# Attention steps of a hybrid decoder layer on one core: the prompt's turn ahead of the cached unit's turn

## The reference

```
# prompt: causal, in blocks of 128 queries, for each of 8 heads
s = (ql @ ckv.T + qr @ krope.T) * scale, masked
o = softmax(s) @ ckv

# sample: 4 new tokens a batch, 8 batches, over 4096 cached rows in pages of 128 and the new rows
s_past = q_lat @ ckv_past.T + q_rope @ krope_past.T
p = softmax(concat(s_past, s_new) * scale)
o = p[:P] @ ckv_past + p[P:] @ ckv_new
```

## Time and profile before

| what | value |
|---|---|
| median of 3 runs | 1400.43 us (1396.89 to 1400.48) |
| the profiled execution: its time | 1402.6 us |
| its span in the profile | 1400.6 us |
| TensorE busy | 1347.0 us, 96% |
| VectorE, ScalarE, GpSimd busy | 44%, 30%, 24% |
| mean granted clock of TensorE | 0.988 of full |

### The profile page before, as it was taken

One profiled execution on the slowest core, in us unless ns is written; L12 is line 12 of the kernel. 1 busy time (PEld: TensorE's weight loads), 2 busy tenths in 40 slices (PEclk: granted clock), 3 DMA queues, 4 the chain that ended last, 5 costly groups with the idle time before them and its releaser, 6 DMA issues.

```text
span 1400.6 us, 28560 instructions
## 1 busy us (share of the span) xinstructions
PE 1347.0 (96%) x11784; PEld 1250.5 (89%) x11784; DVE 614.8 (44%) x1020; ACT 418.0 (30%) x694; POOL 339.6 (24%) x351
## 2 busy tenths in 40 slices
PE   7999999999999999899999988889999999999997
PEld 6999998999999989667777666789999999999997
DVE  6245335234347995334444453355423333333334
ACT  5232221221234222322323333233422222222235
POOL 0219246128221112512222220031121021021022
PEclk9999999999999999999999999999999999999999
DMA  6223222222225213659999976442222222322321
GB/s 234 83 70 104 86 77 78 91 71 82 89 65 181 73 55 98 227 170 308 337 315 329 316 265 209 147 153 91 76 79 87 92 81 83 106 83 68 105 72 67
DMA packets 78932, 189.14 MB, mean 135 GB/s; under 512 B 10226, under 2 KB 13203, under 8 KB 78515
## 3 DMA queue, kind: packets, MB, share of 16 engines
q1 hardware_dynamic: 73762, 176.90, 38.1%
q10 hardware_dynamic: 3024, 6.69, 1.2%
q0 software_dynamic: 2048, 4.20, 0.9%
HBM read 178.06 MB, written 9.69 MB: 134 GB/s over the span
## 4 chain that ended last, share of the span: by engine, by line
PE 84%; DVE 7%; POOL 3%; ACT 2%; issue 2%; DMA 2%; SPq 0%; ACTq 0%; DVEq 0%; POOLq 0%
PE d L1676 59%; PE e L1965 8%; PE e L2018 2%; DVE w_lo L1086 2%; PE e L1999 2%; PE d L2049 2%; PE d L2028 1%; ACT w_hi L579 1%; PE d L2039 1%; PE e L2011 1%; PE e L2002 1%; PE e L1696 1%; PE d L1696 1%; PE e L1844 1%; DMA gate_m<-gates 1%
## 5 line engine op out<-in xcount | busy, mean ns | idle before, releaser
L1086 DVE TENSOR_TENSOR w_lo<-raw,w_hi 128x1024 fp32r<-128x1024 f32 (+2 forms) x191 | 223.6, 1170 | 390.0 <-ACT w_hi L579 389.1
L1676 PE MATMUL d<-x_hi,w_hi 128*128 128x272 f32 x1616 | 337.7, 290 | 9.0 <-DVE w_lo L1296 6.8
L1676 PE MATMUL d<-x_hi,w_lo 128*128 128x272 f32 x1616 | 335.4, 289 | 0.0
L1676 PE MATMUL d<-x_lo,w_hi 128*128 128x272 f32 x1616 | 334.4, 288 | 0.0
L579 ACT CAST w_hi<-raw 128x1024 fp32r<-128x1024 f32 (+2 forms) x191 | 185.7, 972 | 478.2 <-PE d L1676 447.8
L1676 PEld LDWEIGHTS d<-x_hi,w_hi 128*128 128x128 f32 x1616 | 255.4, 189 | 11.5 <-DVE w_lo L1296 6.8
L1676 PEld LDWEIGHTS d<-x_lo,w_hi 128*128 128x128 f32 x1616 | 255.1, 189 | 0.0
L1676 PEld LDWEIGHTS d<-x_hi,w_lo 128*128 128x128 f32 x1616 | 253.5, 190 | 0.0
L937 POOL TENSOR_TENSOR hid<-silu,up 128x544 f32<-128x544 f32 x42 | 56.9, 1356 | 499.3 <-DVE up L1159 487.4
L1676 PE MATMUL d<-hid_hi,w_hi 128*128 128x272 f32 x640 | 134.4, 291 | 4.8 <-DVE w_lo L1086 2.7
L1676 PE MATMUL d<-hid_hi,w_lo 128*128 128x272 f32 x640 | 132.4, 288 | 0.0
(11 more groups left out here) (346 smaller groups left out, 1861.4 us busy)
## 6 DMA issues: line engine op xcount, KB each, us to landing
kv<-kv_src SPq DMA_DIRECT2D x256, 256.0 KB
raw<-w_gu SPq DMA_DIRECT2D x87, 512.0 KB, 3.4
raw<-w_post SPq DMA_DIRECT2D x34, 512.0 KB, 3.4
raw<-w_d1b SPq DMA_DIRECT2D x16, 384.0 KB, 3.2
raw<-w_d2b SPq DMA_DIRECT2D x16, 384.0 KB, 3.2
raw<-w_in SPq DMA_DIRECT2D x10, 512.0 KB, 3.4
gate_m<-gates SPq DMA_DIRECT2D x16, 272.0 KB, 3.7
gates<-gate_m ACTq DMA_DIRECT2D x12, 272.0 KB
```

What stands on the lines that cost most here:

```text
L1086: nc.vector.tensor_tensor(w_lo[:, s % 2, 0:n, :], raw[:, raw_pos(s), 0:n, :], w_hi[:, s % 2, 0:n, :].bitcast(FP), ALU.subtract).then_inc(S ...
L1676: ins = mm(out[:, b, :], w[:, pos, c0 + k, :], x[:, k, b * HALF:(b + 1) * HALF], start=first, stop=stop)
```

## The change

In each step TensorE runs `turn(n - 1)` ahead of `unit_turn(n)` instead of behind it, and ScalarE runs `turned(n - 1)` ahead of `unit_turned(n)`. All else stays: `values(n - 2)` and `unit_values(n)` follow in the same order, and no buffer, wait or load is changed.

```diff
             nc.scalar.activation(p_p[:, n % 2, 0:w], d[:, 0, n % 2, 0:w], ACT.Exp, bias=astat[:, 0, n:n + 1],
                                  accum_out=astat[:, 1, n:n + 1]).then_inc(S.exp_done, 1)
-            unit_turned(n)
             if n >= 1:
                 turned(n - 1)
+            unit_turned(n)
...
             scores(n)
             for k in now[:1]:
                 job(k)
-            unit_turn(n)
             if n >= 1:
                 turn(n - 1)
+            unit_turn(n)
             if n >= 2:
                 values(n - 2)
             unit_values(n)
```

## The result

The changed kernel took 1400.97 us in the median (21 runs) against 1398.85 us (21 runs) of the kernel before, and the measured ratio is 1.0029, 95% interval 1.0016 to 1.0043. The ratio is taken over the fast runs alone, which leaves out one run of the changed kernel (2633.69 us). It is not the quotient of the two medians, which is 1.0015. The forecast of 1.0018 lies between the two and inside the interval, and 1400.97 us lies in the range I gave: the kernel is slower by about 0.3% or less. What the change costs is read from the profiles.

A forecast was written before the change was run, and what follows sets the result against it. TensorE, busy 96% of the span, was taken as the bound. Losses of 0.85 (i=2), 0.22 (n=1) and 1.39 us (n=22, 25, 26, 27) made +2.5 us: 1402.9 us, ratio 1.0018, range 1398.0 to 1406.0.

The forecast's parts named there:

- The chain of 1.07 us: From the unit's turn through copy L802 to the unit's values: 1.07 us that other TensorE work must cover.
- Cover by i: With i = n mod 4 setting block counts: cover suffices at i=0, 1, 3; i=2 short by 0.17 us, n=1 loses 0.22.
- ScalarE's order free: Putting the prompt's copy ahead of the unit's on ScalarE costs nothing itself.
- diag later than the exponentials: At n=22, 25, 26, 27 the prompt's turn waits for diag, 0.1 to 0.4 us behind the exponentials; nothing is hidden.
- rival 3: Waits for the exponentials shrink because the prompt's turn fills them: 1399.8 us, or 1398.2 with full clock at n=27; chance 0.06.
- n=22: Late step where TensorE waits: 0.26 us for diag plus 0.17 for lost cover, 0.43 us together.
- rival 2: Longer idle time at n=22 drops TensorE's clock too: 1404.5 to 1405.5 us; chance 0.16, shared with i=3 losing cover.
- a granted clock below full at n=22: Sign in the profile after that would show the forecast wrong: TensorE's clock below full in step 22.
- n=30 as zero: Step n=30 would add 0.17 us, but counted zero since n=31 waits 0.3 us for kv anyway.
- The lower bound of 1 us: Smallest loss, if a third of the handover is a modelling artefact and later waits take up part.
- L2018's waits at i=2: Sign of being right: the unit's values wait for L802 or ScalarE, 0.1 to 0.2 us each, 1 to 1.5 in all.
- The waits of L2039: Sign of being right: three or four waits for diag replace those for p_n at L2011, over 6.7 us in total.

The follow-up runs named there:

- e4: Changed kernel with values(n-2) also moved ahead of the unit's turn, so all cover is gone: 1425.52 us, ratio 1.0166, loop 287.91 us.
- e8: Changed kernel with the new order on both engines in steps 0 to 21 alone, the old one from 22 on: 1399.97 us, ratio 1.0010.
- e1: The changed kernel run again with no edit: 1405.12 us, ratio 1.0010, loop 268.20 us.
- e2: Kernel before with only TensorE's order changed, ScalarE still copying the unit first: 1406.26 us, ratio 1.0023, loop 268.30 us.
- e3: Kernel before with only ScalarE's order changed, TensorE still running the unit's turn first: 1411.03 us, ratio 1.0060, loop 272.78 us.
- e7: Changed kernel with the new order on both engines in steps 22, 25, 26 and 27 alone: 1399.71 us, ratio 1.0012.
- e10: Changed order with VectorE forming diag of step n early, in step n itself: ratio 0.9975, loop 266.44 us.
- e11: diag formed early on VectorE, new order in steps 22, 25, 26 and 27 alone, old order elsewhere: ratio 0.9987, loop 264.37 us.
- e5: The kernel before, unedited, profiled a second time: 1396.89 us, ratio 0.9997, loop 265.47 us.
- e6: The kernel before, unedited, profiled a third time: one run, 1399.42 us, loop 265.37 us.
- e9: Kernel before, old order, with VectorE forming diag of step n early, in step n itself: ratio 0.9974, loop 265.46 us.
- first pair: First profiles of the kernel before and the changed kernel, no further edit: loop 264.27 us before, 268.26 us after.

## Why the prediction was right, and where not

- **The chain of 1.07 us** was right to 0.01 us: 1.07 between the unit's turn and its values at n=1, 2, 6, 10, 14 and 18 of the changed kernel. It is no constant of the engines, though: behind `values` it was 1.18 (e4).
- **Cover by i** was right: no loss at i=0, 1 and 3, with the 0.05 us of spare at i=3 real, 0.15 to 0.17 us at i=2, 0.21 at n=1. Forecast 1.07 us for these together, measured 1.03; four of the five i=2 steps of e8 give 7.81 to 7.82 again.
- **ScalarE's order free** was right for the pair of edits (e1 against e2), and only for the pair (e3: +8.5 us in the loop).
- **diag later than the exponentials** was right, so rival 3 (faster) fell for the reason given. e7 has +0.43, +0.13 and +0.43 us at n=22, 25 and 26 as forecast; n=27 was +0.35 for +0.40 in the changed kernel (in e7 the clock hides it). e10 and e11 take the reason away, and three of the four steps get shorter in e11, two in e10.
- **The term that was mis-sized** is n=22. The sum has 0.43 us for it, the profile 1.26 and another 0.34 at n=23, 1.2 us too little. That is TensorE's clock. I had this drop as rival 2, 1.6 us on top with a chance of 0.16, and named "a granted clock below full at n=22" as a sign of being wrong. Rival 2's case is what came, at 1.2 us, and the forecast time holds all the same because 1.2 us is small against the range; that is luck. The drop came in all the profiles of the new order on TensorE throughout (after, e1, e2), and in e10 at n=22 and 23 (0.94 and 0.87).
- **Its reason was wrong.** Rival 2 made the drop hang on the idle time at n=22, 2.17 against 2.43 us. The profiles with the old order in the stream (before, e5, e6, e7, e9, e11) have full clock in step 22, also with 2.43 us; those with added stalls in steps 1 to 21 (after, e1, e2, e3, e4, e8, e10) have the drop, also with the old order and its 2.17 us. In e10 the clock dropped behind an idle time of 1.67 us, shorter than the 2.17 that kept it. So the drop goes with what happens ahead of step 22, not with the length of the idle time in it; whether by the stalls themselves or by the place in time to which they move step 22 was not tested. Nor have I a cause for the share at n=27 (0.70 in e3 and e7, 0.74 in e4, 0.83 to 0.92 in the others) or for the second drop in e1. That the drop follows from the change rather than from chance is likely by seven against six profiles, but the mechanism stays open.
- **n=30 as zero** was wrong by little: n=29 and n=30 together are 0.44 us longer in the first pair; e5 and e6 spread n=29 by 0.8 us on their own, so I give this no cause.
- **The lower bound of 1 us** had no sum behind it, only two reasons without a price. Nothing measured came near it.
- The sum of 2.5 us against 3.2 us in the loop (against the mean of before's three profiles) or 4.0 (first pair), and ratios of 1.0018 against 1.0029 and 1.0010: the terms other than the clock measure 2.4 us together (0.21, 0.82, 0.43, 0.13, 0.43, 0.35), the clock at n=22 and 23 another 1.2.
- What I said the profile would show was wrong in two places: L2018's waits at i=2 don't appear in the view of waits, and the clock at n=22 was below full. The waits of L2039 (9.7 us in four places) are as I said.

## What to carry to other kernels

Of two dependent pairs on one engine, ask which work stands between the producer and its consumer, in its real length, and compare it with the chain through the other engine; what is moved ahead of the producer is no cover any more. Before putting work into a wait, look when its own operand is ready: here the filler's operand came 0.1 to 0.4 us after the thing waited for. Forming it earlier on VectorE gave 0.9974 with the old order (e9) and 0.9975 with the new one (e10): the time lay in the operand, not in the order. When two orders are swapped on one engine, ask of the engine that serves them which copy is needed first: it cost 8.5 us of loop to put the copy needed in this step behind the other (e3), and nothing the other way about (e2).

## What the runs showed of the hardware that I had not expected

- A loss of 0.17 us between matmuls (n=18) does not show as a wait: the last matmul's length covers 0.07 us of it, and the 0.10 us left is not listed. Only start-to-start distances show it.
- Full clock or a drop in step 22 went with what lay in the 170 us ahead of it, stalls below a microsecond and the shift of 1 us or more that they make, and not with the length of the idle time in it: 7.45 us at full share with 2.43 us idle time (e7), 7.89 at 0.88 with 2.17 us (e8), 7.17 at 0.94 with 1.67 us (e10).
- Two executions of nearly the same code differ by up to 9.5 us ahead of the loop: its start lay between 596.0 and 605.5 us in all profiles here. VectorE's wait at L1518, where it adds the mask to scores of TensorE, was 8.17 us in the profile after, released by TensorE:

```profile
580.03 0.41 DVE L1518 TENSOR_TENSOR s_new<-e,newmask 32x256 f32<-32x256 f32 x1 [8.17 <-PE e L1944]
```

and 14.96 us in that of before, with a releaser that the profile only calls remote:

```profile
588.83 0.41 DVE L1518 TENSOR_TENSOR s_new<-e,newmask 32x256 f32<-32x256 f32 x1 [14.96 <-remote]
```

In the thirteen profiles it was 8.17 us five times, 10.3 to 10.4 three times and 14.9 to 15.0 five times, with no relation to the edits: the kernel before had 14.96, 8.17 (e5) and 10.38 (e6). The 6.8 us between the shortest and the longest are the greater part of the 9.5. What the longer waits wait for is not shown.
